# First mixture of experts: each weight chunk fetched by four DMAs of a quarter of its columns

## The chip, the cores and the metric

One core of one Trainium2 chip runs the whole kernel as one program. The metric is device time in microseconds (us). Five engines are named as in the profile: PE (TensorE: matmuls, and PEld its weight loads), DVE (VectorE), ACT (ScalarE), POOL (GpSimd) and SP (SyncE, which here only issues DMAs). The core has 16 DMA engines.

## The reference

Two transformer blocks are computed in float32 on 256 tokens of width 1024. The first block has two layers: sliding-window attention with a dense feed-forward, then forgetting attention with a mixture of 8 experts, of which each token uses 2. The second block has a hybrid mixer and a second mixture of 32 experts. The change touches only the mixture of the first block:

```python
def moe_swiglu(x, w_router, b_router, w_in, w_out):
    logits = (x2 @ w_router) + b_router
    top_vals, top_idx = lax.top_k(logits, TOP_K)          # 2 of 8
    gates = jax.nn.softmax(top_vals, axis=-1)
    ...
    def expert_block(args):                                # for each expert
        xb, e = args
        h = xb @ w_in[e]                                   # 1024 -> 2 * 2816
        return (jax.nn.silu(h[:, :D_FF]) * h[:, D_FF:]) @ w_out[e]   # 2816 -> 1024
    ...
    y = zeros.at[slot_tok].add(ys * slot_gate[:, None])
```

One expert has 5632 columns of input weights with 1024 rows, and 1024 columns of output weights with 2816 rows.

## The kernel before

Each engine has one program, written out in order; engines meet only at semaphores. All large weights go through one ring in SBUF, `ringbuf`, of `RING = 4` slots (L26), each of `SLOT = 4096` float32 columns on 128 partitions, that is 2 MB (L28). The list `plan` (L399 to L443) has every chunk in the order of use: its name, its source in DRAM, its columns, and the PE event after which its slot is free. `Chunks` (L135) assigns chunk i to slot i mod 4 and works out the value that the slot's semaphore has once it has landed: 16 for each DMA (L144).

In the first mixture `plan` has, for each of 8 experts, 11 chunks `ein` of input weights (4096 columns: a row of 16 KB for each partition) and 8 chunks `eout` of output weights (2816 columns: a row of 11 KB). That is 152 of the kernel's chunks. In DRAM each chunk is laid out as it will stand in SBUF, one contiguous row for each partition.

SP's program issues the chunks (L2586 to L2595): for chunk i it waits until PE has finished with chunk i - 4, and starts one DMA for the whole chunk. No other engine issues a DMA during the mixture's loop.

PE's program for the mixture (L848 to L881): for each expert, 11 chunks `ein`, where for each chunk 4 groups of 128 hidden units are multiplied with the gathered tokens `XG` (L861; 80 slots for each expert, 64 output rows to an instruction, two instructions side by side); then the tokens of the next expert are gathered (L869, in `gather`, L813 and L818); then 8 chunks `eout` (L878). The results of the expert before are turned (L845) and scattered back (L831, through `one`, L583) between the first chunks of the next one. `take` (L585) makes PE wait for a chunk's semaphore before its first matmul. The profile counts two MATMUL and two LDWEIGHTS for each `pe.matmul` of float32: one chunk `ein` is 128 matmuls in the profile, one chunk `eout` 88. ACT and DVE take the results from PSUM (L2291, L1334).

The stage lies between about 671 and 1480 us of the span. Ahead of it stand the two attentions and the dense feed-forward, behind it the hybrid mixer and the second mixture, which has a ring of seven slots and its own plan (`plan2`, `ring2`).

Of the kernel before, what the change touches and what calls it, by code (L numbers as in the profile page):

```python
# [103 lines left out]
class Sig:  # L104


    def __init__(self, sem, names):
        self.sem, self.names, self.n = sem, list(names), 0
        self.place = {n: i + 1 for i, n in enumerate(self.names)}
# [25 lines left out]
class Chunks:  # L135


    def __init__(self, plan, slots, sems):
        self.plan, self.slots, self.sems, self.taken = plan, slots, sems, 0
        self.value = []  # L140
        count = {}
        for i, (name, src, n, free) in enumerate(plan):
            s = i % len(slots)
            count[s] = count.get(s, 0) + 16 * (src.shape[1] if len(src.shape) == 4 else 1)  # L144
            self.value.append((sems[s], count[s]))

    def dst(self, i):
# [32 lines left out]
def build(nc, dr, out, dbg=None):  # L180
    ctx = ExitStack()
    with ctx:
# [5 lines left out]
        def sem(name):  # L188
            return ctx.enter_context(nc.semaphore(name))
# [25 lines left out]
        def ar(at, *shape):  # L215
            n = int(np.prod(shape))
            assert at + n <= 23500, (at, n)
            a = AR[:, at:at + n]
            if len(shape) == 2:
                return a.rearrange("p (a b) -> p a b", a=shape[0])  # L220
            if len(shape) == 3:
                return a.rearrange("p (a b c) -> p a b c", a=shape[0], b=shape[1])
            return a
# [72 lines left out]
        s_ring = [sem(f"s_ring{i}") for i in range(RING)]  # L296
# [102 lines left out]
        plan = []  # L399
# [48 lines left out]
            for i in range(2):  # L448
                plan2.append(("e2out", dr["e2out"][q, i], SLOT, dnP.at((2, q, i))))
        slots1 = [ringbuf[:, i * SLOT:(i + 1) * SLOT] for i in range(RING)]  # L450
        ring = Chunks(plan, slots1, s_ring)
        ring2 = Chunks(plan2, [ar(23500 - (i + 1) * SLOT, SLOT) for i in range(3)]
                       + [slots1[(n1 + i) % RING] for i in range(RING)], s_ring2)

# [2128 lines left out]
        def sync_program(sp):  # L2583
            at = [0]

            def chunk():  # L2586
                i = at[0]
                if i >= RING:
                    sp.wait_ge(*plan[i - RING][3])
                sp.dma_start(ring.dst(i), plan[i][1]).then_inc(ring.value[i][0], 16)  # L2590
                at[0] += 1

            def chunks_to(i):
                while at[0] < i:
                    chunk()  # L2595

            def gains(k):
                sp.dma_start(GB[:, :], dr["gb"][k]).then_inc(s_g, 16)

            def normed(st):  # L2600
                sp.wait_ge(*lnP.at(st))
                sp.wait_ge(*lnD.at(st))

            def overflow(s, flag, n):
                sp.sem_inc(bar, 1)
                sp.wait_ge(bar, 4 * n)
                with sp.register("flag_s_" + s.tag) as reg:
                    sp.reg_load(reg, flag)
                    with sp.If_ne(reg, 0):
                        for i, (_, src, n_, _) in enumerate(s.plan):  # L2610
                            if i >= 3:
                                sp.wait_ge(*s.plan[i - 3][3])
                            dst, sem_ = s.ring.dst(i), s.ring.value[i][0]
                            if len(src.shape) == 4:
                                d4 = dst.rearrange("p (a b n) -> p a b n", a=src.shape[1], b=src.shape[2])
                                for k in range(src.shape[1]):
                                    sp.dma_start(d4[:, k], src[:, k]).then_inc(sem_, 16)
                            elif len(src.shape) == 3:
                                sp.dma_start(dst.rearrange("p (a n) -> p a n", a=src.shape[1]), src).then_inc(sem_, 16)
                            else:  # L2620
                                sp.dma_start(dst, src).then_inc(sem_, 16)
                        sp.wait_ge(*s.acc.at((s.ne - 1, 1, 1)))

            sp.dma_start(CST[:, 0:128], dr["cst"][:, 0:128]).then_inc(s_i, 16)
            sp.dma_start(mem, dr["mem"].rearrange("a (t p) d -> p (a t) d", p=128)).then_inc(s_m, 16)
            chunks_to(1)
            sp.dma_start(x3, dr["x"].rearrange("a (t p) d -> p (a t) d", p=128)).then_inc(s_x, 16)
            chunks_to(2)
            sp.dma_start(POS[:, :], dr["pos"]).then_inc(s_p, 16)
            sp.dma_start(CST[:, 128:], dr["cst"][:, 128:]).then_inc(s_c, 16)  # L2630
            sp.dma_start(VC[:, :], dr["vec"]).then_inc(s_v, 16)
            chunks_to(RING)
            gains(0)
            for k, st in enumerate(("n0", "n1", "n2")):
                chunks_to(ends[k] + RING)
                normed(st)
                gains(k + 1)
            chunks_to([p[0] for p in plan].index("u2") + RING)
            overflow(sec1, flag1[0:1, :], 1)
            chunks_to(ends[3] + RING)  # L2640
            sp.wait_ge(*ydD.at(3))
            gains(4)
            sp.wait_ge(*r3D.at((3, "out")))
            for i in range(3):
                sp.dma_start(ring2.dst(i), plan2[i][1]).then_inc(ring2.value[i][0], 16)
            chunks_to(n1)
            for i in range(RING):
                sp.wait_ge(*plan[n1 - RING + i][3])
                sp.dma_start(ring2.dst(3 + i), plan2[3 + i][1]).then_inc(ring2.value[3 + i][0], 16)
            normed("n4")  # L2650
            gains(5)
            for i in range(3 + RING, len(plan2)):
                sp.wait_ge(*plan2[i - 3 - RING][3])
                sp.dma_start(ring2.dst(i), plan2[i][1]).then_inc(ring2.value[i][0], 16)
            overflow(sec2, flag2[0:1, :], 2)
            sp.wait_ge(*lnP.at("n5"))
            sp.dma_start(out3[:, 0, :], x3[:, 0, :]).then_inc(s_out, 16)
            sp.wait_ge(s_out, 32)
# [112 lines left out]
def program(nc, arrays, dbg=()):  # L2771
    dr = {n: nc.dram_tensor("in_" + n, a.shape, mybir.dt.from_np(a.dtype), kind="ExternalInput").ap() for n, a in arrays.items()}
    out = nc.dram_tensor("out_0", (1, T, D), F32, kind="ExternalOutput").ap()
    d = {n: nc.dram_tensor("dbg_" + n, s, F32, kind="ExternalOutput").ap() for n, s in dbg}
    build(nc, dr, out, d)
# [11 lines left out]
```

## Time and profile before

| | us |
|---|---|
| median of 3 runs | 2337.8 |
| lowest, highest | 2321.68, 2337.98 |
| the profiled execution | 2335.74 |
| its span, first to last instruction | 2333.9 |

The page of the profile gives each engine's busy time, the granted clock of PE in slices, and the traffic of the DMA engines. Other views group the instructions of a stretch by line, follow the chain of work that ended last, and count the DMA packets of a stretch. In the chain, "issue" is time in which the engine waited for nothing that the profile shows. The DMA view names queues: q1 carries the data that SP's program asks for, and q8 carries instructions.

### The profile page before, as it was taken

The page shows a single profiled execution, that of the slowest core. Times are in us where ns is not written, and L with a number is a line of the kernel's source. Part 1 is how long each engine was busy: PE and PEld are TensorE (multiplying, and loading weights), DVE is VectorE, ACT ScalarE, POOL GpSimd, SP SyncE. Part 2 cuts the span into 40 slices and gives each one's busy share as a digit, 9 for nine tenths or more (in the row PEclk, how much of TensorE's full clock was granted, in tenths as well). Part 3 has the DMA queues.
Part 4 walks back from the last instruction along what each step waited for, and adds up shares of the span by engine and source line. Part 5 has one row for each costly group of instructions (what it writes and reads, how often), then busy time and mean ns, then how long its engine had stood idle before and what let it go on. Part 6 is the DMA issues. An engine that isn't in the chain of part 4 may idle for free.

```text
span 2333.9 us, 52100 instructions
## 1 busy us (share of the span) xinstructions
PE 1972.4 (85%) x24286; PEld 1498.5 (64%) x24286; DVE 528.2 (23%) x1274; ACT 264.7 (11%) x647; POOL 230.1 (10%) x406
## 2 busy tenths in 40 slices
PE   8898999799978888898888888699588789978765
PEld 7656884575468787787878778576355558843321
DVE  1532000213221101011010110303545433132213
ACT  1221000112111000000000000112122212110001
POOL 0000000000000000000000000324566720000000
PEclk9778999895779999999999999799787779979998
DMA  6203343331149988889898898431100005439995
GB/s 265 108 36 126 144 149 149 118 129 70 37 172 337 379 328 349 346 332 377 326 364 339 322 367 331 189 126 54 55 37 1 28 28 234 162 129 397 427 427 244
DMA packets 41027, 498.36 MB, mean 214 GB/s; under 512 B 5448, under 2 KB 5984, under 8 KB 7264
## 3 DMA queue, kind: packets, MB, share of 16 engines
q1 hardware_dynamic: 38992, 493.12, 53.7%
q8 instruction: 195, 3.19, 0.5%
q10 hardware_dynamic: 1808, 1.78, 0.2%
q14 instruction: 32, 0.26, 0.0%
HBM read 493.81 MB, written 1.05 MB: 212 GB/s over the span
## 4 chain that ended last, share of the span: by engine, by line
PE 76%; DVE 7%; issue 7%; DMA 7%; ACT 2%; POOL 2%; DVEq 0%; ACTq 0%; SPq 0%; POOLq 0%
PE pb L861 18%; PE pb L574 16%; PE pb L878 9%; PE pb L579 7%; PE pb L583 6%; DMA ringbuf<-in_e2in 4%; PE pb L759 3%; PE pb L670 2%; PE pb L991 2%; PE pb L1269 2%; DVE arena L1334 2%; PE pb L813 2%; PE pb L1004 2%; PE pb L702 2%; DMA arena<-in_e2in 1%
## 5 line engine op out<-in xcount | busy, mean ns | idle before, releaser
L861 PE MATMUL pb<-arena,ringbuf 128*64 128x80 f32 x11264 | 412.8, 234 | 82.3 <-issue 81.9
L861 PEld LDWEIGHTS pb<-arena,ringbuf 128*64 128x64 f32 x11264 | 399.0, 137 | 99.9 <-issue 99.2
L574 PE MATMUL pb<-XT,ringbuf 128*128 128x256 f32 (+1 forms) x1504 | 334.0, 384 | 2.9 <-ACT XT L2118 2.9
L574 PEld LDWEIGHTS pb<-XT,ringbuf 128*128 128x128 f32 (+1 forms) x1504 | 288.3, 192 | 46.1 <-issue 3.1
L878 PE MATMUL pb<-arena,ringbuf 128*64 128x80 f32 x5632 | 209.7, 237 | 36.9 <-issue 35.9
L878 PEld LDWEIGHTS pb<-arena,ringbuf 128*64 128x64 f32 x5632 | 204.2, 140 | 42.6 <-issue 41.3
L1334 DVE TENSOR_TENSOR arena<-arena,pb 128x160 f32<-128x160 f32 (+2 forms) x178 | 64.8, 364 | 734.4 <-ACT arena L2291 451.2
L2521 POOL TENSOR_TENSOR X<-Y,GB 128x1024 f32<-128x1024 f32 x6 | 14.0, 2338 | 1904.6 <-DVE Y L1334 1904.6
L583 PE MATMUL pb<-arena 64*64 64x64 f32 (+2 forms) x1736 | 156.3, 280 | 38.3 <-ACT arena L2452 16.8
L2118 ACT ACTIVATE arena<-pb 128x256 f32<-128x256 f32 (+5 forms) x202 | 85.1, 435 | 767.1 <-PE pb L574 211.6
L583 PEld LDWEIGHTS pb<-arena 64*64 64x64 f32 (+2 forms) x1736 | 92.3, 158 | 112.5 <-issue 59.9
L579 PE MATMUL pb<-ringbuf,arena 128*128 128x512 f32 (+1 forms) x256 | 97.3, 540 | 2.8 <-DVE arena L1334 1.8
L2291 ACT ACTIVATE arena<-pb 128x160 f32<-128x160 f32 x88 | 26.8, 304 | 600.2 <-PE pb L861 600.2
L579 PEld LDWEIGHTS pb<-ringbuf,arena 128*128 128x128 f32 x256 | 48.4, 190 | 50.2 <-issue 46.4
L759 PE MATMUL pb<-ringbuf,arena 128*128 128x512 f32 x176 | 75.7, 592 | 0.0
L1004 PE MATMUL pb<-XT,ringbuf 128*128 128x256 f32 x192 | 73.3, 486 | 1.4 <-ACT arena L2118 1.4
L605 PE MATMUL pb<-cst,X 128*128 128x128 f32 x96 | 23.4, 427 | 57.7 <-POOL X L2521 44.6
L1334 DVE TENSOR_TENSOR arena<-arena 128x256 f32<-128x256 f32 (+3 forms) x136 | 61.8, 456 | 22.5 <-PE pb L1045 10.9
L670 PE MATMUL pb<-arena 64*128 64x256 f32 (+1 forms) x160 | 63.3, 529 | 0.7 <-DVE arena L1334 0.7
L813 PE MATMUL pb<-arena,X 128*64 128x80 f32 (+1 forms) x768 | 54.5, 259 | 9.0 <-DVE arena L1334 3.8
L991 PE MATMUL pb<-XT,ringbuf 128*128 128x256 f32 x224 | 57.1, 400 | 5.2 <-ACT arena L2118 5.2
L813 PEld LDWEIGHTS pb<-arena,X 128*64 128x64 f32 (+1 forms) x768 | 52.6, 166 | 13.6 <-issue 7.1
(278 smaller groups left out, 1765.4 us busy)
## 6 DMA issues: line engine op xcount, KB each, us to landing
ringbuf<-in_ein SPq DMA_DIRECT2D x88, 2048.0 KB, 9.9
ringbuf<-in_eout SPq DMA_DIRECT2D x64, 1408.0 KB, 7.4
ringbuf<-in_e2in SPq DMA_DIRECT2D x17, 2048.0 KB, 30.2
arena<-in_e2in SPq DMA_DIRECT2D x15, 2048.0 KB, 25.9
ringbuf<-in_fin SPq DMA_DIRECT2D x11, 2048.0 KB, 7.9
ringbuf<-in_e2out SPq DMA_DIRECT2D x10, 2048.0 KB, 23.0
ringbuf<-in_wo SPq DMA_DIRECT2D x6, 2048.0 KB, 7.8
ringbuf<-in_gate SPq DMA_DIRECT2D x8, 1536.0 KB, 6.4
```

The source lines that it names most:

```text
L574: ins = pe.matmul(outp, w[:, j, col:col + m], rT[:, j, :], start=j == 0, stop=j == kt - 1)
L579: ins = pe.matmul(outp, aT[:, j, tt * 128:(tt + 1) * 128], w[:, j, col:col + n], start=j == 0, stop=j == kt - 1)
L583: return pe.matmul(o, l, r, start=True, stop=True)
L670: ins = pe.matmul(o, h["q"][:, qt * 128:(qt + 1) * 128], h["k"][:, 0:kw], start=True, stop=not more)
L759: ins = pe.matmul(PB[2 * h + tt][:, :], hT[:, f + j, tt * 128:(tt + 1) * 128], w3[:, j, h * 512:(h + 1) * 512], start=f + j == 0, stop=f + ...
L813: ins = pe.matmul(PB[b][h_, k * n:(k + 1) * n], x3[:, tt, dt_ * 128 + h_.start:dt_ * 128 + h_.stop], PS_[i][:, tt, :], start=tt == 0, stop ...
L861: ins = pe.matmul(PB[b][h_, t * C1:(t + 1) * C1], w3[:, k, t * 128 + h_.start:t * 128 + h_.stop], XG[e % 2][:, k, :], start=k == 0, stop=k ...
L878: ins = pe.matmul(PB[d // 4][h_, (d % 4) * C1:(d % 4 + 1) * C1], w3[:, f, h_], HT[:, f, :], start=f == 0, stop=f == 21)
L991: ins = pe.matmul(PB[5][:, 0:256], w3[:, j, k * 128:(k + 1) * 128], xT[:, j, :], start=j == 0, stop=j == 7)
L1004: ins = pe.matmul(PB[5][:, 0:256], w3[:, j, br * 128:(br + 1) * 128], xT[:, j, :], start=j == 0, stop=j == 7)
L1334: return v.tensor_tensor(o, a, b, op)
L2118: return a.activation(dst, src, ACT.Copy, scale=1.0 if scale is None else scale)
```

## The change

`Chunks` gets a table of how many DMAs a chunk has, and counts 16 for each of them in the value that a slot's semaphore must reach. The ring is built with four for `ein` and `eout`, and SP's program issues that many DMAs for such a chunk, each for a quarter of its columns on all 128 partitions, one right behind the other, on the same semaphore. Wait conditions, order, ring size and all other chunks stay as they are.

```diff
-    def __init__(self, plan, slots, sems):
+    def __init__(self, plan, slots, sems, pieces=None):
         self.plan, self.slots, self.sems, self.taken = plan, slots, sems, 0
+        self.pieces = [(pieces or {}).get(name, 1) for name, _, _, _ in plan]
...
-            count[s] = count.get(s, 0) + 16 * (src.shape[1] if len(src.shape) == 4 else 1)
+            count[s] = count.get(s, 0) + 16 * (src.shape[1] if len(src.shape) == 4 else self.pieces[i])
...
-        ring = Chunks(plan, slots1, s_ring)
+        ring = Chunks(plan, slots1, s_ring, {"ein": 4, "eout": 4})
...
                 if i >= RING:
                     sp.wait_ge(*plan[i - RING][3])
-                sp.dma_start(ring.dst(i), plan[i][1]).then_inc(ring.value[i][0], 16)
+                w = plan[i][2] // ring.pieces[i]
+                for k in range(ring.pieces[i]):
+                    sp.dma_start(ring.dst(i)[:, k * w:(k + 1) * w], plan[i][1][:, k * w:(k + 1) * w]).then_inc(ring.value[i][0], 16)
                 at[0] += 1
```

A quarter of `ein` is 1024 columns, a row of 4 KB on each partition; a quarter of `eout` is 704 columns, a row of 2.8 KB.

## Rows read from the trace of the kernel before

**Rows 1.** The page, busy time and granted clock in 40 slices.

```profile
PE 1972.4 (85%) x24286; PEld 1498.5 (64%) x24286; DVE 528.2 (23%) x1274; ACT 264.7 (11%) x647; POOL 230.1 (10%) x406
...
PEclk9778999895779999999999999799787779979998
```

**Rows 2.** Stretches: length, busy PE, PEld, DVE, ACT, POOL; clock, DMA share, GB/s.

```profile
671.00:1480.00 809.00, 682.05 (x17552) 640.02 (x17552) 78.28 (x211) 43.93 (x120) 0.00 (x0) 0.99 0.88 343
...
864.00:892.00 28.00, 23.19 (x514) 19.78 (x516) 4.89 (x9) 1.50 (x4) 0.00 (x0) 1.00 1.01 427
```

**Rows 3.** PE by line, 671 to 1480: count, busy us, mean ns, idle before, releasers.

```profile
L861 PE MATMUL pb<-arena,ringbuf 128*64 128x80 f32 x11264 | 412.8, 234 | 82.3 <-issue 81.9 <-DVE arena L1590 0.3
L878 PE MATMUL pb<-arena,ringbuf 128*64 128x80 f32 x5632 | 209.7, 237 | 36.9 <-issue 35.9 <-DVE arena L1334 1.1
L583 PE MATMUL pb<-arena 80*128 80x512 f32 x64 | 31.1, 618 | 1.1 <-DVE arena L1671 1.1
L813 PE MATMUL pb<-arena,X 128*64 128x80 f32 x512 | 22.5, 246 | 5.2 <-issue 3.6 <-DVE arena L1657 1.5
```

**Rows 4.** Chain of work, 680 to 740: start, length, what.

```profile
688.50 4.64 PE pb L861 x127
693.14 1.87 issue
695.01 4.65 PE pb L861 x128
699.66 1.87 issue
701.53 4.64 PE pb L861 x127
```

**Rows 5.** DMA, 676 to 1476: packets, MB, share; issues with KB, us to landing.

```profile
q8 instruction: 137, 2.24, 1.0%
...
ringbuf<-in_ein SPq DMA_DIRECT2D x84, 2048.0 KB, 10.0
ringbuf<-in_eout SPq DMA_DIRECT2D x64, 1408.0 KB, 7.4
```

**Rows 6.** DMA queues, 688.6 to 692.6; this is the only queue there.

```profile
q1 hardware_dynamic: 109, 1.70, 105.4%
```

**Rows 7.** DMA queues, 692.5 to 693.6, the queue of instructions.

```profile
q8 instruction: 1, 0.02, 5.3%
```

**Rows 8.** Chain of work, 984 to 1012.

```profile
1000.16 9.07 PE pb L861 x255
1009.23 0.48 issue
```

**Rows 9.** DMA queues, 1000.2 to 1001.2; this is the only queue there.

```profile
q1 hardware_dynamic: 1, 0.00, 0.1%
```

**Rows 10.** DMA queues, 1001.3 to 1002.3, the queue of instructions.

```profile
q8 instruction: 1, 0.02, 5.9%
```

**Rows 11.** Chain of work, 864 to 892.

```profile
870.04 1.43 issue
...
882.02 1.60 issue
```

**Rows 12.** DMA issues, 864 to 892.

```profile
ringbuf<-in_ein SPq DMA_DIRECT2D x4, 2048.0 KB, 12.2
```

**Rows 13.** DMA, 10.9 to 12.9: rows of 4 KB (`x`).

```profile
DMA packets 208, 0.88 MB, mean 440 GB/s; under 512 B 5, under 2 KB 5, under 8 KB 204
```

**Rows 14.** DMA, 7 to 10: rows of 16 KB.

```profile
DMA packets 77, 1.26 MB, mean 421 GB/s; under 512 B 0, under 2 KB 0, under 8 KB 0
```

**Rows 15.** DMA, 17.7 to 18.7: mostly rows of 1 KB (`pos`).

```profile
DMA packets 176, 0.37 MB, mean 366 GB/s; under 512 B 29, under 2 KB 152, under 8 KB 152
```

**Rows 16.** SP's queue, 0 to 10: start, us, instruction.

```profile
3.96 0.43 SPq L2630 DMA_DIRECT2D cst<-in_cst  x1
4.44 0.45 SPq L2631 DMA_DIRECT2D vec<-in_vec  x1
...
6.67 2.43 SPq L2598 DMA_DIRECT2D GB<-in_gb  x1
```

## The prediction

> **What bounds the kernel now.** I read the page first, then the stretches, then PE by line, then the chain of work through the stage that the change touches, and last the DMA packets at single moments of that chain. On the page PE is busy 85% of the span and no other engine over 23% [rows 1]. The reader is to see that PE sets the time, and that slices 13 to 25, the first mixture, have a clock of nine tenths or more throughout.
>
> The stretches narrow this: from 671 to 1480 us, 809 us, PE is busy 682 us at a granted clock of 0.99, and the DMA engines move 343 GB/s [rows 2]. So 127 us of the stage are not PE work. In the same view, from 864 to 892 us, the DMA engines moved 427 GB/s with a share of 1.01. That is what they can do; 343 is not their limit over the stage.
>
> PE by line tells whose the 127 us are [rows 3]: 81.9 before L861, 35.9 before L878 and 3.6 before L813, all "issue". That makes 121.4 us in which no semaphore, no other engine and no landed chunk is named. The waits that do have a name are about 4 us.
>
> The chain shows their form [rows 4]. PE does 127 or 128 matmuls in 4.64 us, stops for 1.87 us, does 128 more, stops for 1.87 us. 128 matmuls with their 128 weight loads are 256 instructions. The DMA view has a queue of instructions, q8, with 137 packets of 16 KB (2.24 MB) in this stage [rows 5], and the stage's 17552 matmuls and 17552 weight loads are 137 times 256 [rows 2]. So each stop is at the end of one packet of instructions: PE has run out of code. One cycle can be read closely. PE resumes at 688.50 [rows 4]. Until 692.6 only q1 has packets [rows 6], and one of q8 starts between 692.6 and 693.6 [rows 7]; PE resumes at 695.01 [rows 4]. The fetch was thus some 4.1 us in coming, and from there to the next matmul it took some 2.4 us: 6.5 us, where the code lasts 4.64.
>
> How long does it take with quiet DMA engines? PE resumes at 1000.16 [rows 8]. In the next microsecond q1 has one packet of no size [rows 9], and by 1001.3 a fetch is there [rows 10]: 1.15 us. PE then does 255 matmuls, two packets of code, with no stop [rows 8]. With 2.4 us behind it that cycle is 3.6 us, under 4.64. The difference between the two, 6.5 less 3.6, is 2.9 us of waiting behind weights.
>
> Behind how much? Not behind all that is queued: from 864 to 892 the engines are full and a chunk takes 12.2 us to land [rows 12], yet the stops are 1.4 and 1.6 us [rows 11], a wait of about 2.6 us. At 427 GB/s over 16 engines [rows 2] each moves 26.7 KB in a microsecond, so 2.6 to 2.9 us are 70 to 77 KB: four to five rows of 16 KB, of the eight rows that each engine has of a chunk (128 partitions over 16 engines). The fetch waits for a few rows, or for the rest of the DMA that is running on its engine.
>
> The Trainium skill, DMA: Bandwidth & Descriptors, section "Queues, rings and completion order", says that each DMA engine changes between queues only when it has drained a packet of typically 9 to 17 descriptors of one. By that rule a fetch waits for up to a whole DMA's share of its engine, and that share becomes a quarter. The trace's 2.6 to 2.9 us are inside that. The Trainium skill, Runtime: NRT & Kernel Launch, section "Instruction fetch mechanics", describes blocks of 256 instructions on a DMA queue of their own, whose cost is "mostly hidden". The trace agrees on the blocks and not on the cost, 121 us; the sum goes by the trace, and by that page's word it would be 0 gained.
>
> **The change, part by part.** *Rows of a quarter.* If what stands ahead of a fetch is a number of rows, or the rest of one DMA, the wait shrinks to a quarter: 2.6 to 2.9 us become 0.65 to 0.75, the cycle 4.2 to 4.35 us, under 4.64. The stops go, all 121 us. If it is a number of bytes or a time, nothing goes. The trace can't settle this. The nearest row for another size is L878, whose chunks have rows of 11 KB: 35.9 us over 5632/128 = 44 packets of code, 0.82 us each, against 81.9 over 88, 0.93 us each, at L861 [rows 3]. That is less, as a number of rows would have it, but by too little, and half of L878's matmuls run while the 16 KB rows of the next expert are loaded. I take the quarter, because a count of rows or of DMAs is what the two cases have in common best, and keep both ends: 121 us and 0.
>
> *What the stage then costs.* PE's 682 us are one floor. The other is DMA: 88 chunks of 2.097 MB and 64 of 1.442 MB are 276.8 MB, at 427 GB/s [rows 2] 648 us. They are close, and chunk by chunk DMA is the slower one: 2.097 MB take 4.91 us where PE takes 4.64 [rows 4], 1.442 MB take 3.38 us where PE takes 88 times 36.3 ns = 3.19. That is 11 times 0.27 and 8 times 0.19, 4.5 us for an expert, 36 us for eight, if nothing of it is made up. The matmuls that load no weights, L583, L813 and their kind (31.1 and 22.5 us [rows 3]), let DMA catch up, but only by the four slots of the ring. So 0 to 36 us come back as waits for chunks; I take 26, nearer to the upper end, since a slot that comes free also waits for its DMA to start.
>
> *Smaller rows on the DMA engines.* At the start of the kernel rows of 4 KB moved at 440 GB/s [rows 13] and rows of 16 KB at 421 [rows 14]; I take no cost. Rows of 2.8 KB are not in the trace; the nearest from below are rows of 1 KB, at 366 GB/s [rows 15]. Were all weights that slow, the stage would take 276.8/0.366 = 756 us, 53 less than now. So row size alone can't make the stage slower.
>
> *Four issues for one.* 152 chunks get 456 more issues on SP. Back to back an issue takes 0.43 to 0.45 us and follows the last after 0.48 [rows 16]: four are 1.9 us, under the 3.19 us of the fastest chunk. SP has nothing else to do in the stage; behind a late issue stands only the next chunk. The first quarter starts as early as the whole chunk did, and each lasts 1.2 us on the engines, more than the 0.48 to the next, so the data isn't held up. When much is queued an issue can block: 2.43 us at 6.67 us [rows 16]. Then the engines have work, and it costs nothing. Price 0; if that cover is gone, see the slower rival. ACT and DVE follow PE and are idle most of the stage [rows 2].
>
> **Sum.** Against the profiled execution's own time, 2335.7 us (2.1 under the median of 2337.8, inside 2321.7 to 2338.0): 2335.7 - 121 + 26 = 2241 us, 4.1% less. I round to 2240.
>
> **The rivals.** *A count of bytes.* What lies ahead of a fetch is 70 to 77 KB in whatever rows. For it: the small difference between L861 and L878. The stops stay, DMA isn't the bound, and nothing changes: 2336 us, within 1%.
>
> *The gain is taken back in part.* The stops go, but DMA at 366 GB/s [rows 15] becomes the bound: 756 us and some 20 for starts, 33 less than now: 2303 us. The stage needs only fall under 400 GB/s for this to start. For it: the last row of a chunk now comes with the fourth DMA. Against it: 440 GB/s with 4 KB rows [rows 13].
>
> *Slower: the start of each DMA takes room on the engines.* If the 0.328 us or more that SP needs for an issue are not beside the data but between them, 608 DMAs of at least 0.33 us add 200 us to the 648: 848 us where the stage has 809, so 2375 us. This decides from (809 - 648)/608 = 0.26 us for each DMA. For it: the smallest row [rows 15] is also the slowest. Against it: the DMAs of the start, issued 0.48 us apart [rows 16], ran at 421 to 440 GB/s [rows 13, 14].
>
> The Trainium skill, DMA: Bandwidth & Descriptors, section "Bandwidth", speaks against the change: it asks for DMAs of at least 1 MiB for three quarters of the peak, and the quarters are 512 and 352 KB. Its fit, 2.0 us and bytes over 436 GB/s for each DMA, would be, by an estimate from that page with nothing overlapped, 3.2 us for a quarter of `ein`, and the stage would be slower by far more than in my rival. The DMAs of the start overlap, so the trace doesn't bear it out.
>
> **How the numbers follow.** Stops gone, 2215 (all 121 us) to 2285: 0.57. In part, 2285 to 2314: 0.11. Bytes, nothing changed, within 1% (about what a measurement can tell from no change): 0.20. Slower by over 1%: 0.12. So faster 0.68, same 0.20, slower 0.12. The likeliest case has 2215 to 2285 as its own range; 8 times in 10 need the second and nearly all of the third too: 2215 to 2350.
>
> **What would show it.** Right: "issue" before L861 and L878 falls from 118 us to under 20; the stage is about 715 us long at over 380 GB/s; in its place PE shows waits on `ringbuf<-in_ein` of 10 to 40 us; the chain has runs of over 128 matmuls of L861. The bytes rival: the stops of 1.4 to 1.9 us are still there every 128 matmuls. The slower one: waits for chunks at L861, and less than 343 GB/s. SP's issues should be 0.33 to 0.5 us each. The prediction is wrong if the fetch doesn't come sooner, whatever the rest does.

## The result, and the profile after

The changed kernel took 2347.5 us (median of 20 runs, 2334.8 to 2366.4), the kernel before, run beside it, 2333.6 (20 runs, 2314.0 to 2354.2). The ratio is 1.0074, interval 1.0049 to 1.0099: 0.7% slower, where 4% less was forecast. In the profiled executions the spans are 2345.6 and 2333.9 us, 11.7 apart.

The stretches of the kernel after, with the columns of [rows 2]:

```profile
671.00:1480.00 809.00, 670.96 (x17437) 630.89 (x17434) 74.83 (x204) 43.25 (x119) 0.00 (x0) 0.99 0.92 337
```

In the same 809 us PE is busy 671 us instead of 682, at the same clock, and the DMA engines move 337 GB/s instead of 343, with a share of 0.92 instead of 0.88. The engines take more time for fewer bytes. PE by line, as in [rows 3] (an edit above them moved each line by one):

```profile
L862 PE MATMUL pb<-arena,ringbuf 128*64 128x80 f32 x11264 | 414.0, 234 | 89.8 <-issue 89.4 <-DVE arena L1591 0.3
L879 PE MATMUL pb<-arena,ringbuf 128*64 128x80 f32 x5632 | 207.1, 234 | 43.5 <-issue 42.4 <-DVE arena L1335 1.0
```

The stops are not gone; they grew from 81.9 and 35.9 us to 89.4 and 42.4. These 14 us are the 11.7 of the span and a little more. No wait for a chunk has come in their place. The chain of work from 680 to 740 us, where [rows 4] stood:

```profile
687.38 4.64 PE pb L862 x127
692.02 1.59 issue
693.62 4.65 PE pb L862 x128
698.26 1.32 issue
699.59 4.64 PE pb L862 x127
```

The form is the same: one packet of instructions, a stop, the next packet. The DMA view, 676 to 1486 us (beside [rows 5]):

```profile
DMA packets 85686, 275.14 MB, mean 340 GB/s; under 512 B 9499, under 2 KB 9499, under 8 KB 85275
...
q1 hardware_dynamic: 85541, 272.83, 91.5%
q8 instruction: 137, 2.24, 1.1%
...
ringbuf<-in_ein SPq DMA_DIRECT2D x336, 512.0 KB, 7.5
ringbuf<-in_eout SPq DMA_DIRECT2D x256, 352.0 KB, 4.9
```

The change does what it says: 336 DMAs of 512 KB, nearly every packet under 8 KB, and the same 137 fetches. One cycle, to set beside the one read in the prediction: PE resumes at 687.38, and the DMA queues from 691.2 to 692.2 us show

```profile
q1 hardware_dynamic: 104, 0.38, 93.5%
q8 instruction: 1, 0.02, 5.9%
```

with no packet of q8 from 687.4 to 691.2. The fetch still came some 4 us after PE resumed, and the cycle took 6.2 us. It had been 6.5, and the unloaded one is 3.6.

### The profile page after: what moved, and what is told of

It reads as the page before. It is cut to its first block, busy times and chain, and to the rows that moved or that the text cites. A ratio compares the mean times of both kernels' runs of the same rounds, so it can differ in the third digit from the quotient of the medians.

```text
span 2345.6 us, 52556 instructions
## 1 busy us (share of the span) xinstructions
PE 1968.1 (84%) x24286; PEld 1494.6 (64%) x24286; DVE 527.7 (22%) x1274; ACT 264.4 (11%) x647; POOL 229.2 (10%) x406
## 3 DMA queue, kind: packets, MB, share of 16 engines
q8 instruction: 195, 3.19, 0.5%
## 4 chain that ended last, share of the span: by engine, by line
PE 75%; issue 7%; DVE 7%; DMA 7%; ACT 2%; POOL 2%; DVEq 0%; ACTq 0%; SPq 0%; POOLq 0%
PE pb L862 18%; PE pb L575 15%; PE pb L879 9%; PE pb L580 6%; PE pb L584 6%; DMA ringbuf<-in_e2in 4%; PE pb L760 3%; PE pb L671 2%; DVE arena L1335 2%; PE pb L992 2%; PE pb L1270 2%; PE pb L1005 2%; PE pb L814 2%; PE pb L703 1%; DMA arena<-in_e2in 1%
## 5 line engine op out<-in xcount | busy, mean ns | idle before, releaser
L862 PE MATMUL pb<-arena,ringbuf 128*64 128x80 f32 x11264 | 414.0, 234 | 89.8 <-issue 89.4
L862 PEld LDWEIGHTS pb<-arena,ringbuf 128*64 128x64 f32 x11264 | 400.3, 138 | 107.4 <-issue 106.6
L879 PE MATMUL pb<-arena,ringbuf 128*64 128x80 f32 x5632 | 207.1, 234 | 43.5 <-issue 42.4
L879 PEld LDWEIGHTS pb<-arena,ringbuf 128*64 128x64 f32 x5632 | 200.3, 138 | 50.5 <-issue 49.2
L2292 ACT ACTIVATE arena<-pb 128x160 f32<-128x160 f32 x88 | 26.7, 303 | 615.3 <-PE pb L862 615.3
L1335 DVE TENSOR_TENSOR arena<-arena 128x256 f32<-128x256 f32 (+3 forms) x136 | 61.3, 452 | 22.5 <-PE pb L1046 10.9
L606 PEld LDWEIGHTS pb<-cst,X 128*128 128x128 f32 x96 | 19.0, 224 | 65.4 <-POOL X L2522 50.1
```

The source lines that it names most:

```text
L862: ins = pe.matmul(PB[b][h_, t * C1:(t + 1) * C1], w3[:, k, t * 128 + h_.start:t * 128 + h_.stop], XG[e % 2][:, k, :], start=k == 0, stop=k ...
L879: ins = pe.matmul(PB[d // 4][h_, (d % 4) * C1:(d % 4 + 1) * C1], w3[:, f, h_], HT[:, f, :], start=f == 0, stop=f == 21)
L1335: return v.tensor_tensor(o, a, b, op)
```

## The experiments

They answer four questions: are the stops fetches that wait behind weights; what unit is the wait counted in; can the wait be made shorter; and where do the 0.7% come from.

### Are the stops fetches behind weights?

**Quiet engines.** The kernel before, one DMA for a chunk, but only the first quarter of each chunk's columns.

```diff
-                sp.dma_start(ring.dst(i), plan[i][1]).then_inc(ring.value[i][0], 16)
+                w = plan[i][2] // (4 if plan[i][0] in ("ein", "eout") else 1)
+                sp.dma_start(ring.dst(i)[:, 0:w], plan[i][1][:, 0:w]).then_inc(ring.value[i][0], 16)
```

> The kernel before, but of each weight chunk of the first mixture only the first quarter of the columns is loaded, by one DMA; the rest of the slot keeps old data, so three quarters of these weights are not the right ones. The work of PE is the same. Theory (the stops are instruction fetches that wait behind weight data on the DMA engines): with 69 MB in place of 277 a fetch seldom finds a full engine, the stops before L861 and L878 fall from 118 us to under 15, and the stage from 809 to about 700 us. Rival (PE needs the pause of itself at every 256 instructions, whatever the traffic): stops stay near 118 us, stage near 809.

Measured: 2170.2 us. PE by line, then its chain from 680 to 740 us:

```profile
L861 PE MATMUL pb<-arena,ringbuf 128*64 128x80 f32 x11264 | 394.3, 233 | 1.0 <-issue 0.7 <-DVE arena L1590 0.3
L878 PE MATMUL pb<-arena,ringbuf 128*64 128x80 f32 x5632 | 196.9, 233 | 2.4 <-issue 1.3 <-DVE arena L1334 1.1
```

```profile
679.99 44.34 PE pb L861 x1282
```

The same instructions ran 1282 matmuls without a stop. So PE needs no pause of its own, and the load on the DMA engines makes the stops: 2.0 us are left (one execution, but 165 us faster). The busy time fell too, by 31 us, from 412.8 and 209.7 us [rows 3] to 394.3 and 196.9. 44.34 us over 1282 is 34.6 ns a matmul, where the pieces between stops of [rows 4] have 4.64 us over 127 or 128, 36.4 ns. The matmuls themselves are not slower: one takes 233 to 234 ns from start to end in both kernels, and the next starts some 35 ns after it. Only the last one before a stop has no other beside it, and its 0.2 us count as busy. For PE they are lost like the stop, so the stops cost 118 + 31 us rather than 118.

**Half the load.** As above, with half of the columns.

> The kernel before, but only the first half of the columns of each chunk of the first mixture is loaded, by one DMA; the other half of these weights is old data, so not the right ones. Theory (bytes ahead in the engine): a chunk is now 64 KB for an engine and passes in 2.5 of 4.6 us; a fetch finds at most 64 KB ahead and often none. Stops 10 to 50 us, between the 2 us with a quarter of the load and the 118 us with all of it. Rival (fixed time whenever memory is busy): about half of the fetches wait as long as before, stops about 60 us.

Measured: 2204.6 us. Its waits of PE in the stage, and the share of the weights' queue from 676 to 1400 us:

```profile
PE pb L861 <- issue: 6.1, 10, 1.7
...
PE pb L878 <- issue: 2.2, 4, 1.1
```

```profile
q1 hardware_dynamic: 22176, 146.81, 59.6%
```

At 59.6% load there are 14 stops left of the 92 before, 8.3 us in all, under the 10 to 50 expected and far under the rival's 60. They don't shrink with the load in proportion. That fits a stop that appears only once the fetch's wait outgrows the slack of 4.64 less 3.6 us.

**Fewer instructions.** One matmul of 128 rows of weights in place of two of 64, so half the code for the same data (the edit shown, and the same one at L878).

```diff
-                            for h_ in HALF:
+                            for h_ in (slice(0, 128),):
...
```

> The kernel before (one DMA to a chunk), but the expert matmuls at L861 and L878 use all 128 output rows in one instruction where there were two of 64 side by side: half the instructions, so half the fetches, for the same result. A pair of halves takes 72.6 ns now. Theory (PE waits for instructions): if a full matmul also takes about 73 ns, 256 instructions last 9.3 us, over the 6.5 of a slow fetch, so the stops go nearly all, 118 us, some 25 us come back as waits for chunks, and the time is about 2245 us. If a full matmul takes 100 ns or more, PE's own time eats the gain and the time stays near 2335 or above, with no stops either. Rival (stops don't come from the number of instructions): stops stay at 1 us for each chunk.

Measured: 2527.8 us, ratio 1.083 (1.080 to 1.087). PE by line:

```profile
L861 PE MATMUL pb<-arena,ringbuf 128*128 128x80 f32 x5632 | 632.0, 275 | 0.3 <-DVE arena L1590 0.3
L878 PE MATMUL pb<-arena,ringbuf 128*128 128x80 f32 x2816 | 315.8, 275 | 1.1 <-DVE arena L1334 1.1
```

The stops are gone, but each matmul takes 632.0/5632 = 112 ns where two of the half size took 73 [rows 3]. A packet of code now lasts three times as long, so a fetch of 6.5 us fits in it. The stage is longer too, so that the engines are less full (a share of 0.74 from 671 to 1600 us, 0.88 before); but at 0.60 there were still 14 stops, and here there is none. It supports the mechanism and is no way out.

### What is the wait counted in?

**Two and eight DMAs for a chunk.** The change with another number of pieces.

```diff
-        ring = Chunks(plan, slots1, s_ring, {"ein": 4, "eout": 4})
+        ring = Chunks(plan, slots1, s_ring, {"ein": 2, "eout": 2})
```

> The changed kernel with two DMAs to a chunk, rows of 8 and 5.6 KB. Small-rows theory: a third of the change's extra rows, so a third of its extra time, 0.2 to 0.3%, stops 122 to 126 us. If a fetch waited for a number of rows, it would wait half as long as before and the stops would be under 80 us.

> The changed kernel with eight DMAs to a chunk, rows of 2 and 1.4 KB. Small-rows theory: 7/3 of the change's extra rows, so 1.5 to 2.5% over before, stops 145 to 170 us, DMA share of the stage at 0.95 or more. If the extra time is that of the DMAs and issues, the same figure, but then the kernel with four DMAs by partitions is slow too. If a fetch waited for a number of rows, the stops would be gone.

Measured: two pieces 2337.2 us, ratio 1.0023 (1.0000 to 1.0046); eight 2344.7 us, ratio 1.0074 (1.0045 to 1.0104). The waits of PE in the stage, two pieces and then eight:

```profile
PE pb L862 <- issue: 78.5, 65, 2.4
PE pb L879 <- issue: 37.6, 28, 2.4
```

```profile
PE pb L862 <- issue: 63.7, 55, 2.2
PE pb L862 <- DMA ringbuf<-in_ein: 30.3, 7, 5.5
PE pb L879 <- DMA ringbuf<-in_eout: 26.8, 22, 2.8
PE pb L879 <- issue: 2.9, 6, 0.5
```

Had a fetch waited for a number of rows or for the rest of a DMA, two pieces would have cut its wait from 2.9 to 1.5 us and the stops nearly to nothing. Instead the stop of L861's chunks lasts 78.5/65 = 1.21 us with rows of 8 KB, 89.4/65 = 1.38 with 4 KB and 63.7/55 = 1.16 with 2 KB, beside 81.9/66 = 1.24 of before. The row shrank eightfold and the stop stayed. (Nor do the times grow with the number of rows: eight pieces are as slow as four, 0.7%, where 1.5 to 2.5% was expected.) Before L879 the stops did go with eight pieces, but another wait took their place. Its chain at 1058 us shows whose:

```profile
1045.73 12.59 PE pb L879 x353
1058.32 0.34 SPq L2593
1058.66 0.04 issue
...
1059.88 0.43 SPq L2593
```

Eight issues of 0.43 + 0.04 us are at least 3.8 us, and an `eout` chunk is used up in 3.19. SP had become the bound there, and PE waits for weights instead. The DMA engines were not idle meanwhile: from 1046 to 1070 us their share is 0.97, at 305 GB/s. What let the fetches pass isn't shown; by an estimate it is the pace of PE. With 3.8 us for 88 matmuls, 128 take 5.5 us, as long as a packet of code and its stop took in the mean before (4.64 + 0.82).

**Four DMAs of 32 partitions each, whole rows.**

```diff
-                w = plan[i][2] // ring.pieces[i]
+                w = 128 // ring.pieces[i]
                 for k in range(ring.pieces[i]):
-                    sp.dma_start(ring.dst(i)[:, k * w:(k + 1) * w], plan[i][1][:, k * w:(k + 1) * w]).then_inc(ring.value[i][0], 16)
+                    sp.dma_start(ring.dst(i)[k * w:(k + 1) * w, :], plan[i][1][k * w:(k + 1) * w, :]).then_inc(ring.value[i][0], 16)
```

> Four DMAs to a chunk as in the changed kernel, but each has 32 of the 128 partitions with whole rows (16 and 11 KB) in place of a quarter of the columns: the number of DMAs and issues of the change without its small rows. If the change's extra time comes from the small rows (64 thousand more rows with some 8 ns each that the DMA engines pay), this kernel is within 0.2% of the one before, stops 118 to 122 us. If it comes from the number of DMAs (issues, starts, semaphores), it has the change's 0.7% too, stops about 132 us.

Measured: 2796.2 us, ratio 1.200 (1.196 to 1.203). DMA from 700 to 1900 us, and the chain at 1411 us:

```profile
DMA packets 27473, 261.24 MB, mean 218 GB/s; under 512 B 9112, under 2 KB 9112, under 8 KB 9112
...
q1 hardware_dynamic: 27336, 259.06, 99.0%
```

```profile
1411.19 6.29 PE pb L879 x128
1417.47 2.85 issue
1420.33 10.64 PE pb L879 x245
```

This run was meant to tell a count of DMAs from a count of rows, and told something else: engines 99% busy that move half as much. That makes it the best test of bytes against a time. Each engine moved 218/16 = 13.6 KB in a microsecond. The cycle from 1411.19 to 1420.33 is 9.14 us, 5.5 more than the unloaded 3.6: 5.5 times 13.6 is 75 KB. Before, it was 2.6 to 2.9 us at 26.7 KB, 70 to 77 KB. The wait doubled in time and stayed in bytes. (It is one cycle; stops around it give from 55 to 80 KB.)

The packet at 1411.19 takes 6.29 us and not 4.64, because the granted clock fell behind the stop of 3.19 us ahead of it. In the columns of [rows 2]:

```profile
1411.00:1415.00 4.00, 3.81 (x63) 3.81 (x64) 0.00 (x0) 0.00 (x0) 0.00 (x0) 0.57 0.91 211
```

Over the stage the granted clock is 0.86, where it was 0.99 before, so part of the 20% is PE's clock and not the DMA engines.

**A weight source in SBUF.** The kernel after, its weights from the second expert on (chunk 19 of the mixture) copied from a tile in SBUF, in the same quarters, so that the engines write as much and read nothing from DRAM.

```diff
-                    sp.dma_start(ring.dst(i)[:, k * w:(k + 1) * w], plan[i][1][:, k * w:(k + 1) * w]).then_inc(ring.value[i][0], 16)
+                    src = plan[i][1][:, k * w:(k + 1) * w]
+                    if plan[i][0] in ("ein", "eout") and i >= ends[2] + 19:
+                        src = XT[:, 0:w]
+                    sp.dma_start(ring.dst(i)[:, k * w:(k + 1) * w], src).then_inc(ring.value[i][0], 16)
```

> The changed kernel (four DMAs to a chunk, rows of 4 and 2.8 KB), but from the second expert on the weights are copied from a tile in SBUF in place of DRAM, so they are not the right weights, and nearly no data comes from DRAM while the rows, the DMAs and the bytes for each DMA engine stay as they are. Theory (a fetch waits for some 70 KB that stand ahead of it in its own DMA engine, wherever they come from): stops stay, some 0.8 us for each of the 17 packets of instructions of an expert. Rival (the wait is DRAM under load): stops fall to near nothing from the second expert on, about 15 us less for each expert.

Only the stage counts; with other weights the kernel takes another path later (2944.9 us in all). DMA and the waits of PE, 790 to 1390 us:

```profile
q1 hardware_dynamic: 73018, 229.66, 97.4%
```

```profile
PE pb L862 <- issue: 22.8, 40, 1.1
PE pb L862 <- DMA ringbuf<-XT: 7.2, 5, 2.6
PE pb L879 <- issue: 6.9, 14, 0.9
```

Fuller engines than in any kernel with weights from DRAM in quarters (97.4% against 91.5%), yet the stops are 0.57 us long (22.8/40) instead of 1.38. The cycle is 4.64 + 0.57 = 5.2 us, 1.6 over the unloaded one, at 386/16 = 24.1 KB in a microsecond: some 39 KB ahead of the fetch, not 70. Neither theory had this: the amount ahead is not one fixed number of bytes either. It suggests that part of the 70 KB is data asked for from DRAM that has yet to arrive; no run here looks inside an engine, so that stays a suggestion.

**All cycles, not one.** In the kept traces the same reading can be made for every cycle with one packet of code (120 to 129 matmuls from one stop to the next) and one packet of q8 in it. Medians:

| run | cycles | from PE's resuming to the fetch, us | less the unloaded 1.15 | from the fetch to PE's resuming, us |
|---|---|---|---|---|
| before | 69 | 3.8 | 2.7 | 2.3 |
| two pieces | 69 | 3.6 | 2.5 | 2.4 |
| four (after) | 86 | 3.7 | 2.6 | 2.4 |
| eight | 43 | 3.6 | 2.5 | 2.4 |
| 32 partitions each | 78 | 6.7 | 5.6 | 2.8 |
| source in SBUF | 34 | 2.9 | 1.7 | 2.4 |

PE resumes 2.3 to 2.4 us after a fetch starts, whatever came before it (2.8 at half the rate): a stop ends with the fetch. The wait ahead of the fetch is the same for rows of 16, 8, 4 and 2 KB, 67 to 72 KB at 26.7 KB in a microsecond; it is 76 KB at half the rate and 41 KB from SBUF.

### Can the wait be made shorter?

**At most two pieces under way.** SP waits for the last piece but one to land before it issues the next:

```diff
...
+                    if i in landed and len(sent) >= 2:
+                        sp.wait_ge(*sent[-2])
...
```

> The changed kernel, but SP issues a quarter only when the quarter two before it has landed, so that never more than two (64 KB for each DMA engine) are on their way; quarters use two semaphores in turn, so PE has one wait more for each chunk. Theory (bytes queued ahead in the engine): part of the 64 KB has already passed when its landing is told, so a fetch finds 20 to 40 KB ahead, 0.8 to 1.5 us in place of 2.7, and the stops fall from 132 to under 60 us; in exchange two quarters in flight bring only 310 to 375 GB/s, which gives waits for chunks, so that the stage is 760 to 830 us. Rival (a time that doesn't depend on how much is queued): stops stay near 130 us and the waits for chunks come on top, the stage is over 840 us.

Measured: 2822.4 us, ratio 1.212 (1.207 to 1.217). DMA issues from 700 to 1900 us:

```profile
ringbuf<-in_ein SPq DMA_DIRECT2D x327, 512.0 KB, 4.7
ringbuf<-in_eout SPq DMA_DIRECT2D x226, 352.0 KB, 3.5
```

The expectation was far off. A piece takes 3.5 to 4.7 us to land, though at most two are under way, so two at a time feed only 213 GB/s: 2.097 MB take 9.8 us, and PE's cycle on an `ein` chunk is 9.6 (median of 54). The views put 250.2 and 112.8 us of its waits down to "issue", but these are not fetches: PE resumes 5.6 us after the fetch started and not 2.4, and on `eout` chunks it stops after 88 matmuls, where a chunk ends and not a packet of code. They are waits for weights, on two semaphores here, without a name. So the run says nothing of shorter stops. The fetch itself came no sooner, 4.2 us after PE resumed. In the quiet kernel a 512-KB DMA already took 3.8 us:

```profile
ringbuf<-in_ein SPq DMA_DIRECT2D x84, 512.0 KB, 3.8
```

**One engine without weights.** Each chunk as a DMA of 120 partitions and one of 8 (`ring.dst(i)[0:120, :]`, `[120:128, :]`), meant to leave one of the 16 engines to the fetches.

> Whole rows again. Each chunk comes by two DMAs, one for partitions 0 to 119 and one for the last 8. In the kernel before, the 16th engine to report a chunk is 0.5 us later than the 15th in this stage (median) and 0.1 us in quiet ones, which looks as if all fetches went through one engine that also carries a full share of the weights. Theory: a DMA of 120 partitions is spread over 15 engines, and one of 8 over 8. If the engine that is left out is the one of the fetches, the stops fall from 118 us to under 30, and the time by 40 to 90 us (eight of the engines have 9 rows where all had 8, at least 727 us for the stage). If the fetches use another engine or all in turn, the stops stay at 110 to 150 us and the time is the same or up to 2% longer.

Measured: 2888.6 us, ratio 1.243 (1.238 to 1.249). DMA from 700 to 1900 us:

```profile
DMA packets 20194, 244.08 MB, mean 203 GB/s; under 512 B 3055, under 2 KB 3055, under 8 KB 3055
```

The rate halved as with 32 partitions to a DMA, and PE waited for chunks. The fetches were not spared: in the median of 55 full cycles they started 6.8 us after PE resumed. Which engine serves them, and whether it can be spared, stays open.

**A finer release.** A quarter is issued as soon as PE has used that quarter of the slot's last chunk. For this the columns of `ein` are laid out so that each tile `t` of a chunk is one quarter (in DRAM too), and PE counts its event up after each tile. The core of it:

```diff
-                if i >= RING:
-                    sp.wait_ge(*plan[i - RING][3])
...
+                for hi, _ in pieces[i]:
+                    if i >= RING:
+                        sp.wait_ge(*next((p[1] for p in pieces[i - RING] if p[0] >= hi), pieces[i - RING][-1][1]))
+                    sp.dma_start(ring.dst(i)[:, lo:hi], plan[i][1][:, lo:hi]).then_inc(ring.value[i][0], 16)
+                    lo = hi
```

Three forms ran together: quarters, halves, and the layout and the extra events alone, with the slot released as a whole.

> Quarters as in the changed kernel, but also freed and issued one at a time: PE signals each quarter of a chunk when it has read it, and SP issues the quarter that goes there at once, in place of four in a burst after the whole chunk. The input weights stand in DRAM with the 128 columns of each of the four groups together, so that a quarter is what PE reads next; the output weights are cut after 6, 12 and 17 of their 22 rows of blocks. Theory (a fetch waits for the weight bytes that its engine has already taken on, up to 66 to 74 KB, whatever the size of the rows): while DMA keeps up, an engine now has 32 KB or less ahead, 1.2 us, so the fetch cycle is 3.6 to 4.8 us and the stops fall from 134 to 20 to 70 us; some waits for chunks take their place; the time is 2250 to 2310 us, faster than both kernels. Rival (the wait is a fixed time of a loaded memory, whatever is queued): stops stay at 120 to 135 us, the time is 2335 to 2350.

> The same with halves of a chunk (rows of 8 and 5.5 KB), each freed and issued by itself. Theory: an engine has up to 64 KB ahead, but for half of the time less than that; stops between those of the fine release by quarters and those of the kernel before, 60 to 110 us, time 2290 to 2325. Rival (fixed time): as before.

> The kernel of the fine release with its layout, cuts and signals, but SP issues all four quarters of a chunk when PE has finished the whole chunk, as in the changed kernel. Both theories: 2335 to 2355 us, stops 125 to 140 us, as in the changed kernel. If it is faster, the layout made the difference and not the release.

Measured: quarters 2316.9 us, ratio 0.993 (0.990 to 0.995); halves 2310.0 us, 0.991 (0.988 to 0.994); layout alone 2348.6 us, 1.006 (1.003 to 1.010). PE's waits for quarters, then for the layout alone (L879 and L898 are the lines of before's L861 and L878):

```profile
PE pb L879 <- issue: 63.8, 59, 1.9
PE pb L898 <- issue: 37.8, 29, 3.0
```

```profile
PE pb L879 <- issue: 87.1, 65, 3.0
PE pb L898 <- issue: 41.9, 34, 2.2
```

In quarters the finer release is worth 1.3% against the same kernel without it, and makes the one use of small DMAs that pays: both forms are faster than before and after. The gain lies mostly in the stops before the `ein` matmuls and is smaller than expected: 101.6 us of stops and 2316.9 us, where 20 to 70 and 2250 to 2310 were expected. 88 stops remain. That the steadier stream lets more fetches find an engine free is the likely reason and isn't shown by itself. Halves do as well as quarters (the intervals overlap); they have no kernel of their own with the layout alone.

### Where do the 0.7% come from?

The change makes rows smaller and DMAs more at once. **Four DMAs, whole rows:** each takes every fourth partition. **One DMA, small rows:** the weights stand in DRAM as quarters, and one DMA gathers the four.

```diff
-                    sp.dma_start(ring.dst(i)[:, k * w:(k + 1) * w], plan[i][1][:, k * w:(k + 1) * w]).then_inc(ring.value[i][0], 16)
+                    sp.dma_start(ring.dst(i)[k::m, :], plan[i][1][k::m, :]).then_inc(ring.value[i][0], 16)
```

```diff
+                    dst = dst.rearrange("p (q n) -> p q n", q=4)
+                    src = dr[plan[i][0] + "q"][where[i]].rearrange("q p n -> p q n")
```

> Four DMAs to a chunk as in the changed kernel, each with every fourth partition (k, k+4, k+8, ...) and whole rows of 16 and 11 KB; the kernel with four blocks of 32 adjacent partitions ran at half the rate (a row took 1222 ns in place of 611), which hid its question. Small-rows theory: rows and bytes are those of the kernel before, so its time within 0.3% and stops of 118 to 124 us, if every fourth partition doesn't crowd as adjacent ones do. If the change's 0.7% comes from four DMAs in place of one: 0.5 to 1% over before, stops 130 to 136 us.

> One DMA to a chunk as in the kernel before, but the chunk stands in DRAM as four quarters one behind the other, so that the one DMA has 512 rows of 4 and 2.8 KB. Small-rows theory: the change's extra time with one DMA, 0.5 to 1% over before, stops 130 to 136 us, DMA share of the stage 0.92. If the extra time comes from the number of DMAs: within 0.3% of before.

Measured: four DMAs with whole rows 2345.5 us, ratio 1.0056 (1.0028 to 1.0084); one DMA with small rows 2338.1 us, 1.0015 (0.9986 to 1.0045). PE's waits and the weights' queue, first of four DMAs, then of small rows:

```profile
PE pb L862 <- issue: 84.2, 63, 2.4
PE pb L879 <- issue: 42.9, 33, 2.7
...
q1 hardware_dynamic: 28605, 271.31, 89.4%
```

```profile
PE pb L861 <- issue: 81.3, 67, 2.2
PE pb L878 <- issue: 43.8, 31, 3.0
...
q1 hardware_dynamic: 78396, 272.31, 91.0%
```

Two things follow. First, neither a smaller share of a DMA for each engine (four DMAs) nor a smaller row (small rows) shortens the stops, each alone; with that a count of DMAs and a count of rows are both excluded as the unit of the wait. Second, the number of DMAs alone costs a measurable 0.6%, and the small rows alone cost nothing that can be told from zero; but the two intervals overlap, so the runs don't show that the one costs more than the other.

How four DMAs cost it is shown only in part. From 676 to 1480 us the weights' share for each MB is 87.6/275.3 = 0.318 of a per cent before, 0.330 with four DMAs, 0.334 with small rows, and 91.4/270.3 = 0.338 with both: 4, 5 and 6% more engine time for the same data, and in each the stops grow (118 us before; 127, 125 and 132). Busier engines mean fewer free moments for a fetch. But by this measure small rows should cost as much as four DMAs, and their times don't show it; one profile can't settle it. For small rows the packets show where it goes: 159 ns for 4 KB (median), where a quarter of the 611 ns for 16 KB is 153. With four DMAs and whole rows the median stays at 611 ns and the mean grows, from 654 to 664; why is open.

## Why the prediction was wrong, point by point

**What bounds the kernel** was right. PE sets the time, the 121 us of "issue" are its packets of instructions, and they are late because of the weights. The quiet kernel shows it in full (2 us left of 118), and the full-width one, with half the code, agrees. The price was read too low: with the last matmul before each stop, which ends alone, 31 us more.

**The failed step** is "Rows of a quarter". It rested on the sentence that a fetch waits for "a few rows, or for the rest of the DMA that is running on its engine", and chose the quarter "because a count of rows or of DMAs is what the two cases have in common best". What the runs showed in its place is a wait that goes by bytes, about 70 KB on an engine: the same with rows of 16, 8, 4 and 2 KB, with one DMA for a chunk or four, and at half the rate. With the change the fetch came 3.7 us after PE resumed, where it had been 3.8, and the term of 121 us gained came out as 14 lost. (From SBUF it was some 40 KB; what makes up the amount is open.) The bytes rival had it, and had the evidence for it: the stops of L878's 11-KB rows were 0.82 us against 0.93. With a count of rows, 11 KB in place of 16 would have cut a wait of 2.9 us by 0.9, and so nearly ended the stops; 0.11 us was measured. That row weighed more than I let it, and the chance of 0.20 for the rival was too small.

The Trainium skill, DMA: Bandwidth & Descriptors, section "Queues, rings and completion order", led the same way. It says that an engine drains a packet of about 9 to 17 descriptors from one queue before it turns to the next. If that is what a fetch waits for, and each row is a descriptor, the wait must follow the size of a row. The runs from two to eight pieces don't bear that out; the measurement decides.

**What the stage then costs** (26 us of waits for chunks) was never put to the test, since the stops stayed. The waits the prediction named for the right case, on `ringbuf<-in_ein`, did appear with eight pieces: 30.3 us before L862, there with SP's issues in the chain ahead of them.

**Smaller rows at no cost** was right within what can be measured, 0.15% in a kernel of its own. **Four issues for one at no cost** was nearly right and wrong in sign for the result: no quarter came late and no wait for a chunk showed, but four DMAs by themselves cost 0.6%, most of the 0.7% by the medians. Of the slower rival the mechanism fits in kind, more engine time for each DMA, at a tenth of its size: 0.7% of 2336 us over 456 DMAs is 0.036 us for each, where it put 0.33 and decided from 0.26. That cost shows in the stops, not as the bound of the engines that the rival described.

The prediction also set a fit of 2.0 us and bytes over 436 GB/s against the change. It gave that fit under the section "Bandwidth"; in the Trainium skill, DMA: Bandwidth & Descriptors, it stands under "Anatomy of one DMA — SWDGE (gpsimd) path", for DMAs that GpSimd issues, where SP issues these. A 512-KB DMA by itself took 3.8 us here against the fit's 3.2; with many under way the stage was not slowed by more than the 0.7%.

So the time fell into the rival "nothing changes, within 1%", and its 0.7% over the kernel before is the step priced at nothing, four issues for one. That 2347.5 us lies inside the stated 2215 to 2350 is no merit of the sum: the range reached that far only to take in this rival, and the likeliest case ended at 2285.

## What to carry to other kernels

Where PE stops for 1 to 2 us after every 256 instructions with nothing named as releaser, look whether it is out of code: a packet of q8 that starts some 2.4 us before PE resumes says so. Here the DMA engines were why: the fetch waited behind about 70 KB on its engine, and cutting the DMAs up didn't shorten that. What helped is less data, and slots released and refilled in halves or quarters (0.9 and 0.7%). More work for each instruction ended the stops too, but was slower itself. Before a change rests on the unit of a wait, look in the trace for the second size: two sizes that give nearly the same wait speak for bytes or time, not for a count. And "issue" after a wait on two semaphores can be a wait for data, as in the kernel with two pieces under way: see whether the stops fall where a packet of code ends or where a chunk does.

## What the runs showed of the hardware

- How a chunk is cut over the partitions matters far more than into how many DMAs. Every fourth partition: 338 GB/s and +0.6%. Four blocks of 32 adjacent partitions: 218 GB/s with the engines 99.0% busy, +20%. Blocks of 120 and 8: 203 GB/s, +24%. A packet of 16 KB takes 1222 ns with blocks of 32 and 611 before. Engines that are busy at half the rate suggest DMAs that get in each other's way at a place they share; which place isn't shown.
- With quiet engines the fetch starts 1.15 us after PE resumes (one cycle), and by an estimate its code is there after 3.6 us, with the 2.4 that pass from a fetch to PE's next matmul under load. At 60% load it is late now and then (14 stops), at 88 to 92% mostly (92 to 100 stops of 132 packets).
- After a stop of 3.19 us PE's clock was granted at 0.57 for the next 4 us, a mix of its two levels (1.2 and 2.4 GHz); with the shorter stops of the kernel before (1.24 us in the mean before L861) the stage had 0.99.
- One fp32 matmul of 128x128 weights on 80 columns takes 112 ns, two of 128x64 take 73.
- Less data stands ahead of a fetch when the source is SBUF: about 40 KB at 386 GB/s, against 70 to 77 KB.
